# The recurrent branch's Gram products and inverse kept as 64x64 diagonal blocks instead of 128x128 squares

## The chip, the cores and the metric

One Trainium2 chip, one core. The metric is the device time of one execution in microseconds (us), taken as the median of a few runs. TensorE has two clock levels here, 2.4 and 1.2 GHz; a profile gives the granted clock of a stretch as a share of 2.4 GHz.

## The reference

Two different blocks of two layers each, on 256 tokens of width 1024, in float32. The change touches only one branch of the second block's mixer, the recurrent one (`_rwkv7_branch`): eight heads of width 64, each with a 64x64 state that is decayed and updated at every token.

```
def _rwkv7_scan(r, decay, k, v, kk, a):
    def step(state, inp):
        r_t, w_t, k_t, v_t, kk_t, a_t = inp
        sa = jnp.einsum("bhvk,bhk->bhv", state, -kk_t)
        state = (state * w_t[:, :, None, :]
                 + sa[..., None] * (kk_t * a_t)[:, :, None, :]
                 + v_t[..., None] * k_t[:, :, None, :])
        out = jnp.einsum("bhvk,bhk->bhv", state, r_t)
        return state, out
```

Around it, in each of the two layers: one input projection (1024 columns of input, in part for this branch, in part for two convolution branches and for 3072 gate columns), group norm of the branch's output, the gated sum of three branches, an output projection, layer norm, and a feed-forward part (dense in layer 0, a mixture of 8 experts in layer 1). The first block (attention, gates, feed-forward with a convolution) comes before all this and is not touched.

## The kernel before

Weights are streamed in units of 1 MB by SyncE's queue into a ring of buffers. Each engine runs one list of instructions in order, and the engines meet through semaphores: `T.done(...)`, `A.done(...)`, `V.done(...)`, `G.done(...)` count finished work of TensorE, ScalarE, VectorE and GpSimd, and `wait_ge(*V.of("inv", l, p, lv, g))` waits for a certain count. `Z` is one large SBUF tensor that the branch's tiles (`a_`, `b_`, `k_`, `r_`, `gram`, `inv`, `tri`, `off`, `lev`, `xs`, `us`, `state`) are cut from, so a profile calls all of them `Z`. `banks[0..7]` are the eight PSUM banks, all called `bank`.

The recurrence is computed in chunks of 64 tokens. Two chunks make one block `p` of 128 tokens, and there are two blocks (`p` = 0 and 1) in each of the two layers `l`. One block goes through three stages on TensorE (function `rwkv`):

1. **The Gram products** (L841 to L844 and L847). For each head `h` (0 to 7), keys and queries of the 128 tokens are multiplied with each other: four products of 128x128 (contraction over the head's 64 rows) into one bank of 512 columns, and a fifth, L847, which is the transposed one that the inverse starts from. Heads 0, 2, 4, 6 lie in rows 0 to 63 of their tiles and heads 1, 3, 5, 7 in rows 64 to 127. Two banks take turns, so head `h` waits until VectorE has evacuated head `h - 2` (L1931, 512 columns, times a mask that zeroes everything outside the two 64x64 diagonal blocks). L1940 evacuates the fifth product of four heads at a time.
2. **The inverse** of a unit triangular matrix by doubling, in five levels `lv`, for two groups `g` of four heads. GpSimd first prepares it: three operations for each group (L2257, L2259, L2262: 128x512 each) and then `off`, a masked copy of the Gram product for each level (L2268, 128x512). In each level TensorE forms `off.T @ tri` (L862) for both groups; ScalarE copies it out of PSUM into `lev` (L1356, 128x512); TensorE forms `inv.T @ lev` (L870, not in the last level) and `lev.T @ inv` (L873); VectorE adds these to `tri` (L1947) and to `inv` (L1949), 128x512 each. The next level's L862 waits for this.
3. **The chunks**, one after the other (`c` = 0 to 3, two in each block). L893 (with the state) and L895 (with a Gram product) form the right-hand side, ScalarE copies it into `xs`, L901 applies the inverse, VectorE copies that into `us` (L1977), L907 and L908 form the next state, L913 (with the state), L916 and L917 (with Gram products) form the output, which ScalarE copies out (L1374). A chunk's `xs` and `us` are half empty tiles of 128 rows, which is why L1787 clears both at the mixer's start.

TensorE would stand still in much of this, so the projection's remaining units are cut in halves of 16 records (L580, 256 moving columns) and put between: `fill(GRAM_FILL)` (two halves) behind the Gram products, `fill(LEVEL_FILL)` (one half) behind each level, `fill(CHUNK_FILL)` (one half) in each chunk, and fourteen halves before the Gram products. A unit is two halves. ScalarE's list mirrors this: where TensorE's list finishes a unit, ScalarE's waits for it and evacuates it (L1320, 128x512). VectorE's list holds the convolution branch's work between its parts of the levels: `conf_some(3)` puts three taps (six operations, L1862) behind each group's additions in levels 1 to 4 of `p` = 0; in `p` = 1 come the remaining taps, the first block's group norm (L1880 to L1907) and the short convolution.

Around the start of the Gram stage TensorE's list has (L824 forms eight products whose moving side is 2 columns wide):

```
pe.wait_ge(*V.of("bonus", l))
pe.wait_ge(*V.of("rt", l))
pe.wait_ge(*V.of("at", l))
pe.wait_ge(*A.of("tm", l, 5))
for p in range(TB):
    ...
    fill(GRAM_FILL)
    for lv in range(5):
        ...
```

A float32 matmul of the program is two records in the profile (a PE record and a PEld record each time): L862 has 320 records for the 160 matmuls of 2 layers, 2 blocks, 5 levels and 8 heads. A matmul's shape is written as rows*columns of the stationary side, then the moving side.

## Time and profile before

| | us |
|---|---|
| median of 3 runs | 2763.05 (2758.87 to 2769.2) |
| the profiled execution | 2759.35 |
| its span, first to last instruction | 2757.5 |
| TensorE busy | 2632.2 |
| VectorE busy | 1824.5 |
| ScalarE busy | 1260.0 |
| GpSimd busy | 148.8 |

The mean granted clock is 0.981. The three stages of the recurrent branch run from 999.4 to 1179.3 us in layer 0 and from 1572.3 to 1749.4 us in layer 1, so some 360 us of the span.

### The profile page before, as it was taken

The numbers are of one execution on the slowest core, as the hardware profiler recorded it, in microseconds if no ns is written. First come the engines' busy times: TensorE is split into PE (matmuls) and PEld (weight loads), VectorE is DVE, ScalarE is ACT, GpSimd is POOL, SyncE is SP. The second block draws the span as 40 slices with busy tenths as digits, with TensorE's granted clock in tenths as the row PEclk, the third lists the DMA queues.
The fourth block names the chain that finished last, engine by engine and source line by source line (L and its number), as shares of the span: only waits on it lengthen the run. The fifth ranks groups of instructions, "written<-read, shape, count | busy, mean of one in ns | idle before, by whom it ended". The sixth has DMA issues, their size and how long they took to land.

```text
span 2757.5 us, 39119 instructions
## 1 busy us (share of the span) xinstructions
PE 2632.2 (95%) x15410; PEld 2261.3 (82%) x15410; DVE 1824.5 (66%) x2198; ACT 1260.0 (46%) x1443; POOL 148.8 (5%) x125
## 2 busy tenths in 40 slices
PE   7999999999999999999998999889999999999997
PEld 7886998886898888867998888758888888888886
DVE  6654776753777336545545356349889888988988
ACT  4542444451544311113334211127776776777675
POOL 1100000200000021200000023000000000000000
PEclk9999999999999989999998999989999999999999
DMA  6334453333553421135543211249999999999995
GB/s 247 122 138 153 180 189 121 137 139 107 199 183 138 153 77 48 61 122 199 190 169 123 107 62 47 82 188 358 349 356 344 341 358 346 346 359 344 348 357 210
DMA packets 77027, 558.31 MB, mean 202 GB/s; under 512 B 8672, under 2 KB 8800, under 8 KB 9568
## 3 DMA queue, kind: packets, MB, share of 16 engines
q1 hardware_dynamic: 76032, 551.19, 53.6%
q0 software_dynamic: 864, 5.24, 0.5%
q8 instruction: 97, 1.59, 0.2%
q14 instruction: 34, 0.28, 0.0%
HBM read 555.36 MB, written 1.05 MB: 202 GB/s over the span
## 4 chain that ended last, share of the span: by engine, by line
PE 55%; issue 34%; DVE 7%; ACT 2%; POOL 1%; DMA 1%; SPq 0%; POOLq 0%; DVEq 0%; ACTq 0%
PE bank L605 24%; PE bank L628 6%; PE bank L580 6%; PE bank L656 4%; PE bank L590 4%; DVE yT L1862 1%; PE bank L614 1%; PE bank L862 1%; PE bank L873 1%; DMA cst<-in_cst 1%; PE bank L732 1%; PE bank L716 1%; PE bank L715 1%; DVE ring_lo L1584 0%; PE bank L724 0%
## 5 line engine op out<-in xcount | busy, mean ns | idle before, releaser
L2139 DVE TENSOR_TENSOR w_lo<-ring,w_hi 128x2048 fp32r<-128x2048 f32 x216 | 486.3, 2289 | 54.1 <-ACT w_hi L1440 52.9
L1440 ACT ACTIVATE w_hi<-ring 128x2048 fp32r<-128x2048 f32 x216 | 405.1, 1917 | 20.5 <-PE bank L1037 16.7
L1037 PE MATMUL bank<-w_hi,xe_hi 128*128 128x512 f32 x792 | 311.2, 393 | 1.2
L1505 DVE TENSOR_TENSOR w_lo<-ring,w_hi 128x2048 fp32r<-128x2048 f32 x99 | 226.8, 2291 | 127.4 <-ACT w_hi L1136 125.1
L1037 PE MATMUL bank<-w_lo,xe_hi 128*128 128x512 f32 x792 | 308.7, 390 | 0.0
L1037 PE MATMUL bank<-w_hi,xe_lo 128*128 128x512 f32 x792 | 308.3, 389 | 0.0
L605 PE MATMUL bank<-x_hi,w_hi 128*128 128x256 f32 x1056 | 300.4, 284 | 1.5 <-DVE x_lo L1496 1.5
L605 PE MATMUL bank<-x_lo,w_hi 128*128 128x256 f32 x1056 | 300.0, 284 | 0.0
L605 PE MATMUL bank<-x_hi,w_lo 128*128 128x256 f32 x1056 | 299.9, 284 | 0.0
L1136 ACT ACTIVATE w_hi<-ring 128x2048 fp32r<-128x2048 f32 x99 | 189.4, 1913 | 220.4 <-DMA ring<-in_stream 114.8
L580 PE MATMUL bank<-xT,ring 128*128 128x256 f32 x1088 | 251.7, 390 | 1.1 <-ACT Z L1363 1.1
L580 PEld LDWEIGHTS bank<-xT,ring 128*128 128x128 f32 x1088 | 210.5, 196 | 35.0 <-issue 3.4
L605 PE MATMUL bank<-x_hi,ring_lo 128*128 128x256 f32 x832 | 236.9, 285 | 0.0
L605 PEld LDWEIGHTS bank<-x_hi,w_hi 128*128 128x128 f32 x1056 | 203.8, 193 | 3.5 <-DVE x_lo L1496 2.4
L605 PEld LDWEIGHTS bank<-x_lo,w_hi 128*128 128x128 f32 x1056 | 203.9, 193 | 1.1
L605 PEld LDWEIGHTS bank<-x_hi,w_lo 128*128 128x128 f32 x1056 | 203.8, 193 | 0.0
L605 PE MATMUL bank<-x_hi,in_hi 128*128 128x256 f32 x608 | 180.9, 298 | 5.9 <-DVE x_lo L1496 4.5
L1037 PEld LDWEIGHTS bank<-w_hi,xe_hi 128*128 128x128 f32 x792 | 148.6, 188 | 36.5 <-DVE w_lo L2139 6.4
L1037 PEld LDWEIGHTS bank<-w_lo,xe_hi 128*128 128x128 f32 x792 | 148.7, 188 | 31.4
L1037 PEld LDWEIGHTS bank<-w_hi,xe_lo 128*128 128x128 f32 x792 | 148.8, 188 | 30.2
L605 PE MATMUL bank<-x_lo,in_hi 128*128 128x256 f32 x608 | 172.6, 284 | 0.0
L1062 PE MATMUL bank<-w_hi,hT_hi 128*128 128x512 f32 x396 | 163.4, 413 | 0.0
(347 smaller groups left out, 5142.4 us busy)
## 6 DMA issues: line engine op xcount, KB each, us to landing
ring<-in_stream SPq DMA_DIRECT2D x431, 1024.0 KB, 4.9
yT<-in_stream SPq DMA_DIRECT2D x54, 1024.0 KB, 6.2
xT<-in_stream SPq DMA_DIRECT2D x27, 1024.0 KB, 6.6
Z<-in_stream SPq DMA_DIRECT2D x8, 1024.0 KB, 8.7
norm_rows<-in_rows POOLq DMA_DIRECT2D x4, 1024.0 KB, 6.5
cst<-in_cst SPq DMA_DIRECT2D x1, 2145.0 KB, 19.7
par<-in_par SPq DMA_DIRECT2D x1, 1502.0 KB, 15.1
xres<-in_x SPq DMA_DIRECT2D x2, 512.0 KB, 5.9
```

The source lines that it names most:

```text
L580: r = mm(bank[:, c * SEQ:(c + 1) * SEQ], wv[:, k, c * P:(c + 1) * P], xk[:, k, :], start=(k == 0), stop=(k == KT - 1))
L590: r = mm(banks[2 * tb + half], src(c)[:, tb * P:(tb + 1) * P], wv[:, c, half * 512:(half + 1) * 512], start=(first and c == 0), stop=(last ...
L605: r = mm(bank[:, c * SEQ:(c + 1) * SEQ], w[a][:, at], x[b][:, k, :], start=(k == 0 and a == b), stop=(k == KT - 1 and a == 1))
L614: r = mm(bank[:, tb * SEQ:(tb + 1) * SEQ], x[b][:, k, tb * P:(tb + 1) * P], w[a][:, k * 256:(k + 1) * 256], start=(k == 0 and a == b), sto ...
L628: r = mm(banks[2 * tb + half], a[:, j % 2, c, tb * P:(tb + 1) * P], part(b, n)[:, c * D + half * 512:c * D + (half + 1) * 512], start=(j = ...
L656: r = mm(bank[:, half * SEQ:(half + 1) * SEQ], wv[:, k % 2, col:col + P], yk[:, k, :], start=(k == k_at[b]), stop=(k == k_at[b] + splits[b ...
L1037: r = mm(banks[4 + j % 2], a[:, k, :], moe_part(b, i)[:, q * 512:(q + 1) * 512], start=(k == 0 and a is xe_hi and b is w_hi), stop=(k == K ...
L1062: r = mm(banks[half], a[:, j % 2, c * P:(c + 1) * P], moe_part(b, i)[:, c * D + half * 512:c * D + (half + 1) * 512], start=(j == 0 and c ...
L1136: act_(part(w_hi, n), slot(f0 + n), ACT.Copy).then_inc(*A.done("hi", f0 + n))
L1440: act_(moe_part(w_hi, at), moe_slot(at), ACT.Copy).then_inc(*A.done("moe_hi", at))
L1505: v.tensor_tensor(part(w_lo, n), slot(f0 + n), part(w_hi, n).bitcast(F32), ALU.subtract)\
L2139: v.tensor_tensor(moe_part(w_lo, at), moe_slot(at), moe_part(w_hi, at).bitcast(F32), ALU.subtract)\
```

## The change

Outside the two 64x64 diagonal blocks everything that stages 1 and 2 compute is zero. The change keeps a pair of blocks as a tile of 128 rows and 64 columns (rows 0 to 63 the first chunk's block, rows 64 to 127 the second's):

- Stage 1: for each head pair `t`, each of `b_` and `k_`, each chunk `c` and each parity `odd`, one matmul with a 64x64 stationary side and 128 moving columns (64 of `r_`, 64 of `a_`), written to quadrant (rows by parity, output partitions by chunk). Eight heads fill four banks, two heads in each, so VectorE evacuates four times 128x512 (not eight). The transposed products are 16 matmuls of 64*64 with 64 moving columns; they come last and reuse banks 0 and 1, behind a wait for VectorE's first two evacuations; their two evacuations are 128x256.
- Before stage 1 of `p` = 1 TensorE waits for the state of chunk 1 and for ScalarE's copy together; it waited for the state only at the second head.
- Stage 2: `tri`, `inv` and `lev` are 64 columns wide for each head, `off` stays 128 wide and 128x512 for each group. A 128x128 block-diagonal form of `inv` and of `lev` is needed as the stationary side of the other two products, so there are new tiles `inv_wide` and `lev_wide`. Their blocks are copied one at a time (64 rows, 4x64 columns): `inv_wide` at the start by ScalarE (two copies for each group, behind its `fill(GRAM_FILL)`), then by VectorE in levels 0 to 3 (two more additions for each group); `lev_wide` by ScalarE in each level (two copies for each group, next to the one into `lev`). TensorE's first level waits for ScalarE's copies too. `inv` alternates between two buffers. GpSimd's three preparing operations are 128x256.
- Stage 3: the Gram and inverse matmuls take the chunk's 64 rows (64*64) instead of 128 rows with zeros (128*64), with the same 64 moving columns. The matmuls with the state keep all 128 rows (128*64) and 128 moving columns, in the same places between them.
- VectorE's two clearing operations of `xs` and `us` (L1787, 128x512 each) at the mixer's start go; two of 128x1024 (`inv_wide`, `lev_wide`) come just before its part of stage 1, behind its copy of `bonus`. The constants' tensor is 192 columns (98 KB) smaller.

The numbers of fill halves and their places are the same.

```
 # TensorE
-                    for h in range(8):
-                        bs, t = slice(64 * (h % 2), 64 * (h % 2) + 64), h // 2
-                        if h >= 2:
-                            pe.wait_ge(*V.of("gram", l, p, h - 2))
-                        elif p:
-                            pe.wait_ge(*A.of("o", l, 1) if h == 0 else V.of("state", l, 1))
-                            pe.wait_ge(*V.of("us", l, 1))
...
+                    if p:
+                        pe.wait_ge(*A.of("o", l, 1))
+                        pe.wait_ge(*V.of("state", l, 1))
+                        pe.wait_ge(*V.of("us", l, 1))
+                    def quarters():
+                        for c in range(2):
+                            for odd in range(2):
+                                yield c, odd, slice(64 * c, 64 * c + 64), slice(64 * odd, 64 * odd + 64)
+                    for t in range(4):
+                        for wi, w in enumerate((b_, k_)):
+                            for c, odd, ch, bs in quarters():
+                                at = p * P + 64 * c
+                                r = mm(banks[2 * (t // 2) + odd][ch, (t % 2) * SEQ + wi * P:(t % 2) * SEQ + (wi + 1) * P],
+                                       w[bs, t, at:at + 64], r_and_a[bs, :, t * SEQ + at:t * SEQ + at + 64], start=True, stop=True)
+                                if t % 2 and wi and c:
+                                    r.then_inc(*T.done("gram", l, p, t // 2, odd))
+                    for odd in range(2):
+                        pe.wait_ge(*V.of("gram", l, p, 0, odd))
+                    for t in range(4):
+                        for c, odd, ch, bs in quarters():
+                            at = p * P + 64 * c
+                            r = mm(banks[odd][ch, t * 64:t * 64 + 64], a_[bs, t, at:at + 64], b_[bs, t, at:at + 64],
+                                   start=True, stop=True)
...
                     fill(GRAM_FILL)
...
+                                pe.wait_ge(*A.of("inv_wide", l, p, g))
...
-                                r = mm(banks[2 * g][:, (h % 4) * P:(h % 4 + 1) * P], off[:, h, :], tri[:, h, :],
+                                r = mm(banks[2 * g][:, (h % 4) * 64:(h % 4 + 1) * 64], off[:, h, :], tri[:, h, :],
...
-                                    mm(banks[2 * g + 1][:, (h % 4) * P:(h % 4 + 1) * P], inv[:, h, :], lev[:, h, :],
+                                    mm(banks[2 * g + 1][:, (h % 4) * 64:(h % 4 + 1) * 64], inv_wide[:, h, :], lev[:, h, :],
...
+                            pe.wait_ge(*A.of("lev_wide", l, p, lv, g))
...
-                                r = mm(banks[2 * g][:, (h % 4) * P:(h % 4 + 1) * P], lev[:, h, :], inv[:, h, :],
+                                r = mm(banks[2 * g][:, (h % 4) * 64:(h % 4 + 1) * 64], lev_wide[:, h, :], invs[lv % 2][:, h, :],
...
-                                r = mm(dst[:, x * HD:(x + 1) * HD], gram[:, 4 * x + t, 256 + 64 * cc:320 + 64 * cc],
-                                       tm[:, 2, p, t * P + x * HD:t * P + (x + 1) * HD], start=(c == 0), stop=(c == 0 or x == 1))
+                                r = mm(dst[:, x * HD:(x + 1) * HD], gram[ch, 4 * x + t, KA],
+                                       tm[ch, 2, p, t * P + x * HD:t * P + (x + 1) * HD], start=(c == 0), stop=(c == 0 or x == 1))
...
 # ScalarE
                     fill(GRAM_FILL)
+                    for g in range(2):
+                        sc.wait_ge(*G.of("first", l, p, g))
+                        for block, rows in blocks(inv_wide, slice(4 * g, 4 * g + 4)):
+                            act_(block, invs[0][rows, 4 * g:4 * g + 4, :], ACT.Copy).then_inc(*A.done("inv_wide", l, p, g))
...
+                            if lv < 4:
+                                act_(lev[:, hs, :], got, ACT.Copy).then_inc(*A.done("lev", l, p, lv, g))
+                            for block, rows in blocks(lev_wide, hs):
+                                act_(block, got[rows], ACT.Copy).then_inc(*A.done("lev_wide", l, p, lv, g))
...
 # VectorE
-                for buf in (xs, us):
-                    v.memset(buf, 0.0).then_inc(*V.done("zeroed"))
...
+                for wide in (inv_wide, lev_wide):
+                    v.memset(flat(wide), 0.0).then_inc(*V.done("zeroed", l))
...
+                                more = banks[2 * g][:, 0:256].rearrange("p (h n) -> p h n", h=4)
+                                for block, rows in blocks(inv_wide, hs):
+                                    v.tensor_tensor(block, invs[lv % 2][rows, hs, :], more[rows], ALU.add)\
+                                        .then_inc(*V.done("inv_wide", l, p, lv, g))
```

## Rows read from the trace of the kernel before

**Rows 1.** Page, part 1: busy us (share of the span) and instructions
```profile
PE 2632.2 (95%) x15410; PEld 2261.3 (82%) x15410; DVE 1824.5 (66%) x2198; ACT 1260.0 (46%) x1443; POOL 148.8 (5%) x125
```

**Rows 2.** Windows, layer 0: length, busy us (instructions) of each engine, PEclk, DMA
```profile
1000.00:1005.00 5.00, 5.00 (x43) 5.00 (x42) 2.48 (x4) 0.00 (x0) 0.00 (x0) 0.67 0.34 139
...
1040.00:1060.00 20.00, 19.00 (x138) 17.80 (x137) 19.55 (x36) 3.17 (x6) 3.95 (x4) 1.00 0.20 71
...
1107.00:1109.00 2.00, 1.69 (x9) 1.73 (x10) 0.00 (x0) 0.00 (x0) 1.39 (x2) 0.63 0.00 0
```

**Rows 3.** Timeline of TensorE, layer 1, block 0: start, us, instruction, idle
```profile
1572.26 0.49 PE L841 MATMUL bank<-Z 64*128 64x128 f32 x2 [0.27 <-DVE small L1842]
...
1579.85 0.38 PE L847 MATMUL bank<-Z 64*128 64x128 f32 x2
...
1580.16 7.17 PE L580 MATMUL bank<-xT,ring 128*128 128x256 f32 x32
...
1589.64 2.36 PE L862 MATMUL bank<-Z 128*128 128x128 f32 x16 [2.31 <-POOL Z L2268]
```

**Rows 4.** Timeline of TensorE, layer 0, block 1
```profile
1089.88 0.48 PE L841 MATMUL bank<-Z 64*128 64x128 f32 x2 [0.68 <-ACT Z L1374]
...
1090.65 0.27 PE L844 MATMUL bank<-Z 64*128 64x128 f32 x1
...
1091.20 0.38 PE L843 MATMUL bank<-Z 64*128 64x128 f32 x2
...
1097.84 7.17 PE L580 MATMUL bank<-xT,ring 128*128 128x256 f32 x32
...
1107.31 3.56 PE L862 MATMUL bank<-Z 128*128 128x128 f32 x16 [2.29 <-POOL Z L2268]
```

**Rows 5.** Timeline of TensorE, layer 0, block 0
```profile
999.41 0.48 PE L841 MATMUL bank<-Z 64*128 64x128 f32 x2 [0.27 <-DVE small L1842]
...
1010.70 9.46 PE L580 MATMUL bank<-xT,ring 128*128 128x256 f32 x32
```

**Rows 6.** Timelines of GpSimd and ScalarE around stage 1
```profile
1098.31 1.27 POOL L2257 TENSOR_TENSOR Z<-Z,cst 128x512 f32<-128x512 f32 x1 [46.98 <-DVE Z L1940]
...
1587.37 0.60 ACT L1320 ACTIVATE gates<-bank 128x512 f32<-128x512 f32 x1 [16.42 <-PE bank L580]
```

**Rows 7.** Groups of instructions by shape: 256 columns on GpSimd, ScalarE and VectorE
```profile
L2219 POOL TENSOR_TENSOR Z<-Z 128x256 f32<-128x256 f32 x2 | 1.5, 739 | 0.2
...
L1183 ACT ACTIVATE Z<-bank 128x256 f32<-128x256 f32 x2 | 0.7, 364 | 0.0
...
L2148 DVE TENSOR_TENSOR gates<-gates,bank 128x256 f32<-128x256 f32 x99 | 41.1, 415 | 0.0
```

**Rows 8.** Timeline of TensorE: 128-column stationary sides, 2 and 128 moving
```profile
997.30 1.84 PE L824 MATMUL bank<-cst,Z 128*128 128x2 f32 x16
...
1020.00 1.95 PE L862 MATMUL bank<-Z 128*128 128x128 f32 x16
```

**Rows 9.** Timelines of VectorE and TensorE, layer 0, block 0, level 3
```profile
1047.48 0.69 DVE L1947 TENSOR_TENSOR Z<-Z,bank 128x512 f32<-128x512 f32 x1
...
1048.09 0.68 DVE L1949 TENSOR_TENSOR Z<-Z,bank 128x512 f32<-128x512 f32 x1
...
1058.62 1.16 PE L862 MATMUL bank<-Z 128*128 128x128 f32 x8 [0.72 <-DVE Z L1949]
```

**Rows 10.** Timeline of TensorE, layer 0, chunk 2: a tiling change between stages
```profile
1162.27 0.38 PE L908 MATMUL bank<-Z 64*128 64x128 f32 x2
...
1162.59 0.43 PE L913 MATMUL bank<-Z 128*64 128x128 f32 x2
...
1162.86 0.28 PE L916 MATMUL bank<-Z 128*64 128x64 f32 x2
...
1162.97 0.28 PE L917 MATMUL bank<-Z 128*64 128x64 f32 x2
```

**Rows 11.** Chain that ended last, layer 0's mixer start: start, us, what
```profile
884.37 0.48 DVE Z L1787
```

More of the change, by code:

```diff
@@ L148, in const_names @@
                     ("causal", 384), ("window", 384), ("cos64", 256), ("sin64", 256), ("cos32", 256), ("sin32", 256),
-                    ("chunk2", 256), ("earlier", 128), ("slots", 128), ("ones", 128), ("first", 128), ("levels", 6 * 128), ("heads2", 2), ("reset", 256), ("tie", 64)):
+                    ("chunk", 128), ("earlier", 128), ("slots", 128), ("ones", 128), ("first", 64), ("near", 64), ("levels", 5 * 128), ("unit", 64), ("heads2", 2), ("reset", 256), ("tie", 64)):
         n.add(name, w)
@@ L454, in emit, with blocks @@
         rwo = Z[:, 11264:12288].rearrange("p (b n) -> p b n", b=TB)
-        gram = Z[:, 12288:16384].rearrange("p (h n) -> p h n", h=8)
-        inv = Z[:, 16384:17408].rearrange("p (h n) -> p h n", h=8)
-        tri = v_.rearrange("p t n -> p (t n)").rearrange("p (h n) -> p h n", h=8)
+        gram = Z[:, 12288:14336].rearrange("p (h n) -> p h n", h=8)
+        inv_wide = Z[:, 14336:15360].rearrange("p (h n) -> p h n", h=8)
+        lev_wide = Z[:, 15360:16384].rearrange("p (h n) -> p h n", h=8)
+        invs = [x.rearrange("p (h n) -> p h n", h=8) for x in (Z[:, 16384:16896], v_.rearrange("p t n -> p (t n)")[:, 512:1024])]
+        lev = Z[:, 16896:17408].rearrange("p (h n) -> p h n", h=8)
+        tri = v_.rearrange("p t n -> p (t n)")[:, 0:512].rearrange("p (h n) -> p h n", h=8)
         off = Z[:, 17408:18432].rearrange("p (h n) -> p h n", h=8)
-        lev = Z[:, 18432:19456].rearrange("p (h n) -> p h n", h=8)
+        r_and_a = Z[:, 0:12288].rearrange("p (x n) -> p x n", x=2)
+        BR, BA, KR, KA = (slice(64 * i, 64 * i + 64) for i in range(4))
+        def blocks(wide, hs):
+            return [(wide[64 * c:64 * c + 64, hs, 64 * c:64 * c + 64], slice(64 * c, 64 * c + 64)) for c in range(2)]
         xs = Z[:, 19456:19968]
@@ new lines, in rwkv @@
+                    for odd in range(2):
[5 more added lines that the diff above has]
+                                   start=True, stop=True)
+                            if t == 3 and c:
+                                r.then_inc(*T.done("m", l, p, odd))
@@ new lines, in mixer @@
+                    for pair in range(2):
+                        for odd in range(2):
+                            ve.wait_ge(*T.of("gram", l, p, pair, odd))
+                            if p:
+                                ve.wait_ge(*T.of("o", l, 1))
+                            at = 4 * odd + 2 * pair
+                            v.tensor_tensor(gram[:, at:at + 2, :].rearrange("p h (w n) -> p (h w) n", w=2),
+                                            banks[2 * pair + odd].rearrange("p (q n) -> p q n", q=4),
+                                            grow(ct("chunk"), [P, 4, P], 1), ALU.mult).then_inc(*V.done("gram", l, p, pair, odd))
@@ L1942, in mixer @@
+                    for g in range(2):
+                        ve.wait_ge(*T.of("m", l, p, g))
+                        if p == 0 and g == 0:
+                            ve.wait_ge(*A.of("tm", l, 1))
+                        v.tensor_tensor(tri[:, 4 * g:4 * g + 4, :], banks[g][:, 0:256].rearrange("p (h n) -> p h n", h=4),
+                                        grow(ct("first"), [P, 4, 64], 1), ALU.mult).then_inc(*V.done("first", l, p, g))
                     for lv in range(5):
@@ L2255, in mixer @@
                             po.wait_ge(*V.of("ends", l))
-                        ident4 = grow(ct("ident"), [P, 4, P], 1)
+                        ident4 = grow(ct("unit"), [P, 4, 64], 1)
                         g.tensor_tensor(tri[:, hs, :], tri[:, hs, :], ident4, ALU.add).then_inc(*G.done("tri1", l, p, gg))
-                        g.tensor_tensor(inv[:, hs, :], gram[:, hs, 0:P], grow(ct("levels", 0, P), [P, 4, P], 1), ALU.mult)\
+                        inv = invs[0]
+                        g.tensor_tensor(inv[:, hs, :], gram[:, hs, BA], grow(ct("near"), [P, 4, 64], 1), ALU.mult)\
                             .then_inc(*G.done("inv1", l, p, gg))
@@ L2330, in level @@
         return ((lo // (2 * n) == hi // (2 * n)) & (lo % (2 * n) < n) & (hi % (2 * n) >= n)).astype(f)
-    c["first"] = level(1, j, i)
-    c["levels"] = np.concatenate([level(n, i, j) for n in (1, 2, 4, 8, 16, 32)], 1)
+    narrow = lambda m: m[:, 0:64] + m[:, 64:128]
+    c["first"] = narrow(level(1, j, i))
+    c["near"] = narrow(level(1, i, j))
+    c["levels"] = np.concatenate([level(n, i, j) for n in (2, 4, 8, 16, 32)], 1)
+    c["unit"] = narrow((i == j).astype(f))
     c["heads2"] = (i[:, 0:2] // 64 == j[:, 0:2]).astype(f)
```

57 lines of the change are left out of this document (16 added, 41 removed).

## The prediction

> **What bounds the kernel now.** I read the page first: TensorE is busy for 2632 of 2757.5 us [rows 1]. So where its list runs without a gap, only less work on TensorE shortens the time, and elsewhere only the wait that ends last. Then I read the recurrent branch in windows, in time order on each engine, and along the chain that ended last. The reader should see three regimes. Around stage 1 the gap in front of level 0 is ended by GpSimd: 2.31 and 2.29 us [rows 3, 4]. (In layer 0's block 0 the clock hides it, below.) In levels 1 to 4 of block 0 VectorE is busy for 19.55 of 20 us and TensorE waits for it, 0.72 us in front of the last level's second group [rows 2, 9]; so it is in levels 0 to 2 of block 1 by the same timeline. The chunks are one chain with TensorE in nearly all of it. The fill halves are work that has to be done somewhere, so I move them and never save them.
>
> I use five paces, all in records (two for a float32 matmul). A pair of records with a 64*128 stationary side and 128 moving columns takes 0.22 us, 0.111 each. Sixteen records of 128*128 with 128 moving take 1.95 us, the last one's 0.28 included: again 0.111 [rows 8]. Sixteen of 128*128 with only 2 moving columns take 1.84 us, so 0.106 each [rows 8]: with next to nothing to stream, a 128-column stationary side still costs 0.106. With 64-column stationary sides and 64 moving it is 0.056 (L916 to L917, two records in 0.11 us) [rows 10]. And where two heads in different row halves stand next to each other, eight records pass between 1090.65 and 1091.20, 0.069 each against 0.111 [rows 4]: the halves do overlap.
>
> **Stage 1, pace.** Before: 80 records for a block. After: 64 with 128 moving columns and 32 with 64. Every next matmul is in the other row half, so I take a perfect overlap of two: 64 x 0.0555 = 3.55 us and 32 x 0.029 = 0.93 us, 4.5 in all. Bounds: 1.8 + 0.5 us if all four quadrants overlap; 7.1 + 1.8 = 8.9 us if nothing does. The trace has two partners at once and never four, so I take two. VectorE keeps up: its evacuations of 512 follow one another in 0.60 us [rows 9]; pair 0 at 1.9 to 3.2, pair 1 at 3.75 to 5.0, the first 256-wide one done at 5.4. Its two new 128x1024 clearings fall into the 1.9 us before the first evacuation and into idle time before it.
>
> The Trainium skill, page "TensorEngine Tiling (Array Packing)", section Key Properties, says that different tiles load and multiply in parallel, and lists four tiles for 64x64. By that rule stage 1 would take 2.3 us in place of 4.5; no row here shows more than two.
>
> **Stage 1 to level 0.** GpSimd: from its start at 1098.31 to TensorE's at 1107.31 seven operations of 512 take 9.0 us [rows 4, 6]. A 256-wide one took 0.739 us [rows 7], pitch 0.70, so six of them with two own waits take 4.3, and `off` 1.25: 5.45 + 4.3 + 1.25 + 0.15 = 11.15 us after stage 1 began. TensorE has 4.5 + 0.1 (tiling change, below) + 7.17 of fill [rows 3] = 11.8 us. GpSimd is no longer last; its gap goes.
>
> In block 0 something takes its place. ScalarE's list has its own `fill(GRAM_FILL)` ahead of the new `inv_wide` copies. Fourteen halves went before, so these two complete a unit with their last record: its evacuation starts at 1587.37, right at the fill's end [rows 6]. Level 0 then waits 0.6 us for it and for two copies of 64x256 (0.364 each) [rows 7]: 1.4 us with the hand-overs. In block 1 seven more halves lie between, the unit ends in the middle of the fill, and the copies are long done.
>
> - Layer 1, block 0: 17.4 us from 1572.26 to 1589.64 [rows 3]; after, 11.8 + 1.4 = 13.2. L862's sixteen records took 2.36 there against 1.95 [rows 3, 8]. Gain 4.2 + 0.4 = 4.6.
> - Layer 0, block 0: the clock fell in it (mean 0.67 from 1000 to 1005 us) [rows 2]; before, TensorE had done the products of two columns. I assume the same fall, 1.9 us in. 34 records by then, 30 x 0.111 + 32 x 0.058 = 5.2 after, the fill begins at 1006.5 and takes the same 9.4 us [rows 5]: 1015.9 + 1.4 = 1017.3 against 1020.00 [rows 8]. Gain 2.7. With full clock it would be 6 more.
> - Block 1, both layers: 17.4 us [rows 4]; after, 11.8 plus 0.55, since the first product now waits for the last of four state operations. Gain 5.1. Behind the 2.29 us gap the clock was down (0.63 in 1107 to 1109) [rows 2], and L862 took 3.56 against 1.95 [rows 4, 8]; without the gap I give back 1.6. Together 6.7, twice: 13.4.
>
> Sum of this part: -20.7 us.
>
> **Levels.** The moving side is halved, but `off`, `inv_wide` and `lev_wide` are stationary sides of 128 columns. Bounds: 0.056 and 0.111 a record. The nearest row is that of 2 moving columns, 0.106, so I take 0.106: 48 records save 0.24 us in a level, and in eight of the twenty levels TensorE sets the pace: -1.9. VectorE: additions of 512 have a pitch of 0.60 against a duration of 0.69 [rows 9]; a 256-wide one lasts 0.415 [rows 7], so pitch 0.33. Four of these (1.32) replace two of 512 (1.20): +0.12 for each group, and in twelve groups of each layer VectorE sets the pace: +2.9. ScalarE's three copies (1.1 us) instead of one (0.6) are hidden: `lev` is sooner ready, and L870's eight records (0.85) cover the wide copies; in the last level it has 0.85 us for two copies of 0.73. If that cover went, each level would cost up to 0.5 more. GpSimd's `off` is unchanged and still overlaps VectorE's taps.
>
> **Chunks.** Numbers of records and columns stay, so contraction over 64 rows saves nothing. But the tiling does not stay: in chunks 1 to 3 the state products are 128*64 and the Gram products between them become 64*64. L908 (64*128) starts at 1162.27 and lasts a pair's 0.22; L913 (128*64) starts at 1162.59, 0.10 late, and its own pair takes 0.27 instead of 0.22 [rows 10]. A change of rows alone, L847 to L580, costs 0.09 (1579.85 + 0.22 against 1580.16) [rows 3]. Four alternations in each of two stages are 14 new changes for a chunk, 84 in six chunks. Bounds: 0 (if this one pair of tilings mixed freely, which no row excludes) and 0.15. I take 0.15, since every change seen costs: +12.6. All of it lies on the chain, as nothing else waits there but TensorE's own order.
>
> The Trainium skill, same page and section, says that a change of tiling mode, though not one of tile, drains TensorE. By that rule, the rows above agree, with 0.10 us a time.
>
> **Mixer start.** The two clearings of `xs` and `us` (0.48 each, 0.51 with the gap) stand on the chain in front of the first split [rows 11]. ScalarE's high part is ready at about the same time as they start, so I give back 0.95 in each layer: -1.9. The smaller constants I count at nothing.
>
> **Sum.** -20.7 - 1.9 + 2.9 + 12.6 - 1.9 = -9.0 us against the profiled execution's 2759.35. That execution is 3.7 us under the median of the three runs, 2763.05; against the median I forecast 2754.
>
> **Rivals.**
> 1. Four quadrants overlap. Level 0 then starts 10.3 us after stage 1 began instead of 11.8 (VectorE and GpSimd follow close behind): 1.5 us four times and 1 more in the slow stretch, 2747. For it: the quadrants share no row-and-column pair. Against it: only pairs seen. The Trainium skill's rule on tiles, named above, is this case.
> 2. 128*64 and 64*64 mix without a cost: 12.6 less, 2741. For it: both have 64 columns. Against: the change of rows alone cost 0.09.
> 3. The levels run at the moving side's pace: 48 x 0.05 - 0.24 = 2.2 us in eight levels, 2737. Against it: the 0.106 row.
> 4. Slower: the clock. In the levels the array would stream for about half of each record's 0.106 us; if the granted clock falls to 1.2 GHz there as it did at 1001 and 1107 us [rows 2], a level costs 5.1 us more. From five levels on the kernel is slower; in the eight that TensorE paces it would be +41, 2795. Against it: fill stands behind nearly every level, and the chunks' 64-column products, with as few columns in flight, kept the full clock by the same timelines.
> 5. The quadrants give nothing, one after another: +4.4 us four times and some 2 more in the slow stretch, 2774. Against it: [rows 4].
> 6. The change does not shorten GpSimd's preparation (256-wide operations as long as 512-wide): level 0 starts at 14.5 us, +2.7 twice and +1.3 twice, 2762.
>
> **Chances and range.** My forecast 0.48, rivals in order 0.18, 0.08, 0.05, 0.06, 0.10, 0.05. What a measurement here can tell is 0.5%, 13.8 us: under 2749.2 is faster, over 2776.9 slower. Faster: 0.15 of the forecast, two thirds of rival 1, all of rivals 2 and 3: 0.32. Slower: rival 4 mostly and a quarter of rival 5: 0.07. Same: 0.61. Leaving out rivals 3 and 4 and the far edge of rival 5, the range is 2740 to 2771.
>
> **What would show it.** Right: no idle time ended by GpSimd before level 0; in block 0 an idle of about 1.4 us ended by ScalarE; from stage 1's start to level 0 some 12 to 13 us; L862, L870 and L873 of 128*128 with 64 moving at 0.106 a record; steps of 0.15 us wherever 128*64 meets 64*64. Wrong: level records at 0.056, a stage 1 under 3 us, chunks as long as before, or a granted clock near 0.5 in the levels.

## The result, and the profile after

The changed kernel takes 2800.3 us (median of four runs, 2793.27 to 2802.6); before took 2764.8 beside it (2758.87 to 2769.2). The ratio is 1.0126, with a 95% interval of 1.0098 to 1.0153: slower by some 35 us, where the prediction had 9 us less and put the end of its range at 2771. The profiled execution of after is 2793.27 us with a span of 2791.5, 34.0 more than the span of before, and its mean granted clock is 0.965 against 0.981. It is the fastest of the four (the other three have 0.960 or 0.961), so the stretches below show rather too little of the loss than too much.

The page of after, part 1 and the clock row of part 2, answers to [rows 1]; the last line is the clock row of before:

```profile
PE 2661.6 (95%) x15474; PEld 2270.1 (81%) x15474; DVE 1818.6 (65%) x2246; ACT 1282.2 (46%) x1531; POOL 135.3 (5%) x125
...
PEclk9999999999999998899999988889999999999999
...
PEclk9999999999999989999998999989999999999999
```

TensorE does the same fill and fewer columns, and is busy for 29 us more. The clock row says where to look: it has six 8s where before has three, and the new ones stand in the two places where the recurrent branch runs (a digit is some 70 us). So I cut the branch of each layer into three kinds of stretch: from stage 1's first record to level 0's, the five levels, and the two chunks of a block. Each is the difference of two start times, of both layers and both blocks together. (In block 1 the stretch of chunks is taken from its first Gram record. The state product ahead of it, 0.3 us in before and 0.4 in after, stands with the levels.)

| stretch | before | after | change | predicted for it |
|---|---|---|---|---|
| stage 1 to level 0 | 72.8 | 47.9 | -24.9 | -17.1 |
| levels | 182.8 | 198.0 | +15.2 | -2.6 |
| chunks | 101.3 | 138.9 | +37.6 | +12.6 |
| all else | | | +6 | -1.9 |

(Of the prediction's -20.7 for stage 1, 3.6 were for records of the first level, so they stand in the second row here.) "All else" is 3.0 us ahead of layer 0, -1.4 between the two layers and 4.4 behind the second. Layer 0's stage 1 starts anywhere from 999.2 to 1008.1 us in the traces of this study, whatever was changed in them, so the first figure says nothing about this change. Some 2 of the last 4.4 are the clock again, which stays down behind the last chunk: the four records that follow it (L941) take 3.78 us, in before (L922) 1.98. The other 2 are not explained.

The stretches of layer 0 in the windows of after; then narrower ones, around the places where the clock falls (length, busy us and instructions of TensorE, its weight loads, VectorE, ScalarE and GpSimd, granted clock, DMA share and GB/s). They answer to [rows 2]; the last line is the stretch of block 0's chunks in before:

```profile
1002.45:1015.26 12.81, 9.78 (x129) 8.35 (x129) 4.82 (x8) 1.54 (x4) 6.69 (x8) 1.00 0.22 79
1015.26:1064.55 49.29, 47.88 (x304) 44.99 (x304) 34.13 (x81) 11.50 (x32) 10.02 (x8) 0.90 0.17 63
1064.55:1097.63 33.08, 29.26 (x209) 23.70 (x209) 6.11 (x16) 2.97 (x5) 0.00 (x0) 0.79 0.09 33
...
1108.79:1159.98 51.19, 46.97 (x300) 43.57 (x298) 37.05 (x68) 14.58 (x34) 13.52 (x10) 0.90 0.13 49
1159.98:1195.17 35.19, 32.26 (x224) 24.96 (x223) 3.90 (x8) 2.37 (x4) 0.00 (x0) 0.82 0.08 30
...
1071.00:1073.00 2.00, 1.74 (x15) 1.74 (x16) 0.21 (x1) 0.00 (x0) 0.00 (x0) 1.00 0.95 389
1073.00:1075.00 2.00, 2.00 (x20) 1.88 (x20) 1.13 (x4) 0.00 (x0) 0.00 (x0) 0.58 0.25 102
1033.00:1036.00 3.00, 1.59 (x14) 1.45 (x12) 2.90 (x8) 1.62 (x4) 1.27 (x1) 0.96 0.58 177
1036.00:1044.00 8.00, 8.00 (x38) 8.00 (x38) 6.29 (x14) 1.03 (x3) 1.27 (x1) 0.50 0.16 68
...
1065.18:1089.88 24.70, 21.55 (x208) 19.26 (x209) 6.04 (x16) 2.96 (x5) 0.00 (x0) 1.00 0.12 44
```

Block 0's chunks take 33.08 us at a mean of 0.79. In before the same stretch takes 24.7 us at 1.00; by the same windows, before's clock is 1.00 in every stretch of chunks of both layers. That is the finding of this study, and everything below asks what pulls the clock down.

The timeline of TensorE, after, layer 0: stage 1 of block 0 up to level 0 (it answers to [rows 3, 5]), level 2's second group, chunk 0, and the x stage of chunk 2; the last two lines are the x stage of chunk 2 in before (start, us, instruction, idle time before it and what ended that):

```profile
1002.45 1.98 PE L855 MATMUL bank<-Z 64*64 64x128 f32 x64 [0.27 <-DVE small L1866]
1005.83 0.69 PE L864 MATMUL bank<-Z 64*64 64x64 f32 x32 [1.40 <-DVE Z L1959]
1006.46 7.17 PE L589 MATMUL bank<-xT,ring 128*128 128x256 f32 x32
1015.26 1.97 PE L880 MATMUL bank<-Z 128*128 128x64 f32 x16 [1.62 <-ACT Z L1375]
...
1035.37 1.62 PE L880 MATMUL bank<-Z 128*128 128x64 f32 x8 [1.41 <-DVE Z L1979]
1036.78 1.91 PE L888 MATMUL bank<-Z 128*128 128x64 f32 x8
...
1069.28 1.14 PE L920 MATMUL bank<-Z 64*64 64x64 f32 x16
1071.26 0.48 PE L926 MATMUL bank<-Z 64*128 64x128 f32 x2 [0.84 <-DVE Z L2007]
...
1073.24 0.43 PE L935 MATMUL bank<-Z 64*64 64x64 f32 x2
1073.46 0.42 PE L936 MATMUL bank<-Z 64*64 64x64 f32 x2
...
1159.62 0.43 PE L912 MATMUL bank<-Z 128*64 128x128 f32 x2
1159.98 0.44 PE L914 MATMUL bank<-Z 64*64 64x64 f32 x4
1160.35 0.43 PE L912 MATMUL bank<-Z 128*64 128x128 f32 x2
...
1153.59 0.39 PE L893 MATMUL bank<-Z 128*64 128x128 f32 x2
...
1154.04 0.39 PE L893 MATMUL bank<-Z 128*64 128x128 f32 x2
```

Four things to read. First, stage 1's 64 records pass in 1.98 us, a pitch of (1.98 - 0.27) / 63 = 0.027 us: four quadrants at once. Level 0 begins 12.81 us after stage 1, behind an idle time ended by ScalarE's copies. Second, a chunk's stages: the pair L935, L936 has a pitch of 0.21 us, 0.107 a record, where [rows 10] had two records of the same number of columns in 0.11. That is not a change of tiling, since chunk 0 has none between these two: it is the clock, at 0.58 in that window. Third, a change of tiling has its own price: a step from one L912 to the next, four records of L914 and two changes between them, is 0.73 us where before has 0.45 from one L893 to the next for as many records, 0.14 for each change. Fourth, eight records of L888 take 1.91 us in the window at 0.50 and 1.06 at full clock.

VectorE of after just ahead of level 2's second group (level 1's additions for it), the timeline (it answers to [rows 9]):

```profile
1033.66 0.42 DVE L1973 TENSOR_TENSOR Z<-Z,bank 128x256 f32<-128x256 f32 x1
1034.00 0.86 DVE L1977 TENSOR_TENSOR Z<-Z,bank 64x256 f32<-64x256 f32 x2
1034.89 0.42 DVE L1979 TENSOR_TENSOR Z<-Z,bank 128x256 f32<-128x256 f32 x1
1035.23 3.77 DVE L1886 SCALAR_TENSOR_TENSOR yT<-Z,par,yT 128x252 f32<-128x252 f32 x6
```

The group now occupies VectorE from 1033.66 to 1035.23, 1.57 us, where two additions of 512 took 1.21 [rows 9] (from 1047.48 to its next start at 1048.69). The two additions of 64 partitions take 0.43 each, as long as one of 128 partitions: half the partitions save nothing.

ScalarE and GpSimd of after around level 0 of block 0, the timeline:

```profile
1007.29 0.73 POOL L2287 TENSOR_TENSOR Z<-Z,cst 128x256 f32<-128x256 f32 x1 [62.99 <-DVE Z L1966]
...
1013.67 0.60 ACT L1339 ACTIVATE gates<-bank 128x512 f32<-128x512 f32 x1 [12.53 <-PE bank L589]
1014.16 1.72 ACT L1375 ACTIVATE Z<-Z 64x256 f32<-64x256 f32 x4
```

GpSimd's 256-wide operation is 0.73 us and no gap ends with it any more. ScalarE evacuates the fill's unit at the fill's very end, and only then makes the four copies on which level 0 waits.

### The profile page after: what moved, and what is told of

It reads as the page before. It is cut to its first block and busy times, and to the rows that moved or that the text cites. A ratio compares the mean times of both kernels' runs of the same rounds, so it can differ in the third digit from the quotient of the medians.

```text
span 2791.5 us, 39399 instructions
## 1 busy us (share of the span) xinstructions
PE 2661.6 (95%) x15474; PEld 2270.1 (81%) x15474; DVE 1818.6 (65%) x2246; ACT 1282.2 (46%) x1531; POOL 135.3 (5%) x125
```

## Experiments

Two theories stood at first. **The array theory:** TensorE's clock falls where its records use a small part of the array, here the chunks' 64*64 products (A in the expectations); with 128 rows in each product the chunks would go back to full clock. **The other theory (B):** the chunks cost only their changes of tiling, some 12.6 us, and the rest of the loss comes out of the levels. The first two experiments put that part of the change into before, and take it out of after.

**Chunk products on 64 rows, in the kernel before.**

```
-  r = mm(dst[...], gram[:, 4 * x + t, 256 + 64 * cc:320 + 64 * cc], tm[:, 2, p, ...])
+  r = mm(dst[...], gram[ch, 4 * x + t, 256 + 64 * cc:320 + 64 * cc], tm[ch, 2, p, ...])
...
-  r = mm(banks[1][ch, ...], inv[:, 4 * (h % 2) + h // 2, ch], xs[:, ...])
+  r = mm(banks[1][ch, ...], inv[ch, 4 * (h % 2) + h // 2, ch], xs[ch, ...])
...
-  mm(d, gram[:, ..., 128 + 64 * cc:192 + 64 * cc], us[:, hv]); mm(d, gram[:, ...], tm[:, 2, p, hv])
+  mm(d, gram[ch, ..., 128 + 64 * cc:192 + 64 * cc], us[ch, hv]); mm(d, gram[ch, ...], tm[ch, 2, p, hv])
```

> The kernel before with stage 3 alone changed: the Gram and inverse matmuls of the chunks take the chunk's 64 rows (64*64) in place of 128 (128*64). Theory A (small tiles): a chunk of 64*64 matmuls makes the granted clock fall by itself, as it fell in chunk 0 of the changed kernel, where nothing changes its tiling; then this kernel shows the clock near 0.5 from the first chunk on, and is slower than before by about 38 us (12.6 for 84 tiling changes, some 25 for the clock): 2803. Theory B (the clock falls because the shorter stage 1 and the levels' waits leave gaps, and stage 3 costs only its tiling changes): the clock stays at 1.0 in the chunks and the kernel is slower by about 13 us: 2778.

2812.49 us against 2765.35, ratio 1.0166 (1.0145 to 1.0187): 47 us slower from a change of row slices alone, 9 more than the array theory's figure, and slower than the whole change. The levels stay as they were (45.2 and 46.2 us in layer 0, at 1.00 and 0.96). The windows of its chunks of block 0, and the timeline of TensorE in chunk 0:

```profile
1069.35:1103.79 34.44, 31.28 (x209) 25.13 (x209) 6.04 (x16) 2.96 (x5) 0.00 (x0) 0.72 0.08 31
```

```profile
1074.05 1.14 PE L901 MATMUL bank<-Z 64*64 64x64 f32 x16
1076.03 0.48 PE L907 MATMUL bank<-Z 64*128 64x128 f32 x2 [0.84 <-DVE Z L1977]
...
1077.03 0.38 PE L907 MATMUL bank<-Z 64*128 64x128 f32 x2
...
1077.49 0.64 PE L907 MATMUL bank<-Z 64*128 64x128 f32 x2
```

The fall can be watched here: the same form of instruction takes 0.38 us, and half a microsecond later 0.64. Ahead of it stand sixteen 64*64 records, a wait of 0.84 and some 64*128 records. The following stretch pays too: stage 1 of block 1 takes 21.2 us at a clock of 0.74, where before has 17.4 at 1.00.

**After with the chunk products on 128 rows.** The reverse of the diff above, on the changed kernel's tiles; the kernel leaves out keeping the two chunks' products apart.

> The changed kernel with the chunks' Gram and inverse matmuls back on 128 rows (128*64), and the clearing of xs and us back. The compact tiles hold both chunks' blocks, so these products mix the two chunks: the output is not the reference's, the work on every engine has the shape of a correct kernel. Theory A: the chunks keep the full clock and take 24.7 and 26.2 us in layer 0 as before instead of 33.1 and 35.6, and the kernel is about 38 us faster than the changed one: 2762, level with before. Theory B: only the tiling changes go, the clock still falls in the chunks: 2787.

2768.05 us against 2765.35, ratio 1.0011 (1.0000 to 1.0022). That is 32 us less than after: the array theory, by 6 us off its figure. The windows are worth more than the sum: the chunks are at 25.4 and 25.9 us and 1.00 in layer 0, but now the levels of block 1 take 56.9 and 58.2 us at 0.79 and 0.77. So there is a second fall, in the levels, and it moves about: the levels of block 0 are at 1.00 in layer 0 (46.3 us) and at 0.90 in layer 1 (49.3 us) of this one execution. Nor do 128 rows rule the fall out. The chunks of block 0 in layer 1:

```profile
1635.07:1663.45 28.38, 24.56 (x209) 22.25 (x209) 6.10 (x16) 2.96 (x5) 0.00 (x0) 0.88 0.11 38
```

The clock is at 1.00 up to 1641 us there and falls behind the wait of 0.84 and the state products, where the chunks of after lose it too.

**State products first, so that fewer tilings alternate.** The stages x and o issue their four 128*64 products ahead of all Gram products: one change in a stage and not seven. A third theory (C) was at stake, that the alternation brings the clock down.

```
+  if c:
+      for t in range(4):
+          mm(banks[0][ch, t * P:(t + 1) * P], a_[:, t, tc_], state[:, t, :], start=(t == 0), stop=False)
   for t in range(4):
       dst = banks[0][ch, t * P:(t + 1) * P]
-      if c:
-          mm(dst, a_[:, t, tc_], state[:, t, :], start=True, stop=False)
```

> The changed kernel with the four state products of a stage put ahead of its Gram products instead of between them: 12 of the 14 new tiling changes of a chunk go, 72 in all; the same matmuls. Each change is worth 0.15 us, so -10.8 us: 2789, with the clock falling in the chunks as before (theory A, the size of the tiles). If instead it is the tiling changes with their drains that bring the clock down (theory C), the clock stays up in chunks 1 to 3 as well and the kernel comes to about 2770.

2786.5 us against 2765.35, ratio 1.0082 (1.0065 to 1.0099). 14 us less than after, where 72 changes at 0.14 are 10. The third theory falls: with hardly a change left, block 0's chunks still stand at 32.1 us and 0.75.

**Stage 1 with the row halves apart.** All products of one row half first, then the other: no two neighbours in different row halves.

```
-  for t in range(4):
-      for wi, w in enumerate((b_, k_)):
+  for want in range(2):
+      for t, (wi, w) in [(t, q) for t in range(4) for q in enumerate((b_, k_))]:
           for c, odd, ch, bs in quarters():
+              if odd != want:
+                  continue
```

> The changed kernel with stage 1's 64 records of one block in another order: all of rows 0 to 63 first, then all of rows 64 to 127, so neighbours differ only in the output partitions. If four quadrants work independently and only neighbours overlap, the pitch is 0.056 us a record (3.6 us in all, instead of 0.027 and 1.7). If column halves do not overlap by themselves and the four-way pace came from a deep queue, it is 0.111 (7.1 us).

One execution, 2817.87 us. TensorE's timeline, block 0:

```profile
1003.30 3.34 PE L857 MATMUL bank<-Z 64*64 64x128 f32 x64 [0.27 <-DVE small L1868]
```

(3.34 - 0.27) / 63 = 0.049 us a record, against 0.027 with four quadrants and 0.111 for a 64*128 stationary side [rows 4]. Two column halves overlap without the row halves, which the expectation had a little slower. Level 0 of block 0 still starts at 12.8 us, since ScalarE's copies come last; but the clock is down in block 1's stage 1 (15.5 us at 0.68, after has 11.2 at 0.87) and in its levels (58.4 us at 0.77). Less of the array in use at a time, and again the clock; but this is one execution, and the levels' 64 moving columns lose the clock without this edit too.

**Levels with 128 moving columns.** If a half-streamed 128-column stationary side is what brings the clock down in the levels, then streaming the 64 columns twice must mend it, although it is twice the columns. The second copy goes to bank columns that nothing reads.

```
-  r = mm(banks[2 * g][:, (h % 4) * 64:(h % 4 + 1) * 64], off[:, h, :], tri[:, h, :], ...)
+  r = mm(banks[2 * g][:, (h % 4) * P:(h % 4 + 1) * P], off[:, h, :], grow(tri[:, h, :], [P, 2, 64], 1), ...)
```

and likewise for `inv_wide` by `lev` and `lev_wide` by the inverse, the readers taking every other 64 columns.

> The changed kernel with each of the levels' three products streaming its 64 moving columns twice (128 moving columns, the second copy's result unused; the readers take the first). The pitch of a record should stay 0.111 us, as the stationary side sets it. If the clock falls in the levels because the array streams only about half of each record's time, the four level stretches (49.3, 51.2, 46.3, 51.2 us) come to about 46 each with the clock at 1.0: 2785 to 2790. If it falls because of the waits for VectorE there, or carries over from the chunks, nothing changes: 2800.

2779.18 us against 2764.7, ratio 1.0058 (1.0040 to 1.0077): 21 us less than after for twice the moving columns in the levels. Its timeline at the place where after's clock fell at 1035 us:

```profile
1032.12 1.16 PE L880 MATMUL bank<-Z 128*128 128x128 f32 x8 [1.40 <-DVE Z L1979]
1033.12 1.06 PE L888 MATMUL bank<-Z 128*128 128x128 f32 x8
```

The wait ahead is the same (1.40 against 1.41, for the same addition), the records are the same in number and stationary side, and L888's eight take 1.06 us here and 1.91 in after. One such pair would prove little, for after's own layer 1 has the same records behind the same wait and keeps the clock:

```profile
1619.70 1.10 PE L880 MATMUL bank<-Z 128*128 128x64 f32 x8 [1.41 <-DVE Z L1979]
1620.64 1.06 PE L888 MATMUL bank<-Z 128*128 128x64 f32 x8
```

It is the count over all traces that decides. With 64 moving columns the levels of block 0 have a mean clock of 0.90 in eight of ten stretches (after, no_s3, grouped, rows_apart, act_first) and 1.00 in two; with 128 moving columns (this kernel and the five below that keep the edit) they have 1.00 in all twelve. In block 1 it is 0.76 to 0.90 against 0.93 to 1.00. So 64 moving columns make the fall likely behind these waits, not certain. Nor are 128 proof against it: in block 1 of this kernel, behind a wait of 3.58 us, the clock is 0.71 from 1124 to 1126 us. And at full clock the 64 moving columns have given nothing: L888's eight take 1.06 in either kernel.

**The same, with the chunk products on 128 rows too.**

> The same on the kernel with the chunks back on 128 rows (output not the reference's: the two chunks' products are mixed). Its level stretches were 46.3, 56.9, 49.3 and 58.2 us against 46 each before. If the moving columns are what holds the clock, they come to 46 each and the whole gain of stage 1 shows: 2765 - 25 = 2740. If the waits are the cause: 2768.

2744.5 us against 2764.7, ratio 0.9923 (0.9905 to 0.9940). With both edits undone, stage 1's gain is left: 20 us. The predicted gain of stage 1 was real. Seven of its eight stretches of levels and chunks in question are at 0.96 or above; the chunks of block 1 in layer 1 are at 0.94, with a fall behind the state products again.

**Idle twins.** The change keeps the diagonal blocks alone, so the chunks' products stay at 64 rows and the array must be filled in another way. Each Gram product of x and o gets a neighbour in the opposite quadrant (the other rows, the other columns), whose output nobody reads, on top of the two edits above (128 moving in the levels, state products first). No run has those two alone, so what the twins add to the whole kernel is an estimate: 2779.2 less grouped's 13.8 would be 2765.

```
   for x in range(2):
+      ot = slice(64 - 64 * cc, 128 - 64 * cc)
+      mm(banks[1][ot, ...], gram[ot, 4 * x + t, KA], tm[ot, 2, p, ...], start=True, stop=True)
       r = mm(dst[...], gram[ch, 4 * x + t, KA], tm[ch, 2, p, ...], ...)
```

> lev128, the state products grouped ahead, and beside each 64*64 Gram product of the chunks' x and output stages an idle twin of the same size in the opposite quadrant (other row half, other output partitions, a free bank; its result is unused). If the quadrants overlap as in stage 1, the twins cost little (0 to 2 us in a chunk); if the clock falls in the chunks because only a quarter of the array works, it falls less or not at all: 2760 to 2770. If the clock does not depend on that share, it stays down and the kernel is at 2775 or above.

2754.76 us against 2764.7, ratio 0.9963 (0.9949 to 0.9977). Block 1's chunks are at 25.8 us and 1.00. Block 0's are not (30.3 at 0.83), and the windows say why:

```profile
1066.00:1068.00 2.00, 1.16 (x13) 1.02 (x12) 0.68 (x1) 0.00 (x0) 0.00 (x0) 1.00 0.71 238
1068.00:1070.00 2.00, 2.00 (x22) 1.78 (x21) 0.38 (x2) 0.00 (x0) 0.00 (x0) 0.71 0.68 287
1070.00:1072.00 2.00, 2.00 (x42) 2.00 (x42) 0.74 (x3) 0.00 (x0) 0.00 (x0) 0.50 0.03 8
```

The clock falls behind the inverse's records and the state products, which have no twins yet.

**A fill half in place of twins.** On the same two edits, half a unit of fill between the state update and o, one in each chunk; they are taken from the fourteen halves ahead of the Gram products (thirteen now) and from behind the last chunk.

```
   r.then_inc(*T.done("s", l, c))
+  fill(1)
```

> lev128, the state products grouped ahead, and one more fill half in each chunk, between the state's and the output's products, taken from the halves that ran before stage 1 and behind the last chunk. The work is the same. If a stretch of small tiles without full-array work in it makes the clock fall, a fill half in its middle keeps it up: 2755 to 2765. If the small tiles bring it down whatever stands between: about 2775.

2760.65 us against 2764.7, ratio 0.9985 (0.9975 to 0.9995). Block 0's chunks are at 1.00 (33.0 us, with two more fill halves of 3.6 us in them), block 1's at 0.86 (37.9 us). Fill that would have to be done anyway can hold the clock too, though here only in one block of two. That small tiles bring the clock down whatever stands between them is ruled out by block 0.

**Twins for the inverse and the state products too.**

```
   for h in range(8):
+      mm(banks[3][ot, h * 64:h * 64 + 64], invs[1][ot, h, :], tm[ot, 2, p, h * 64:h * 64 + 64], ...)
       r = mm(banks[1][ch, h * 64:h * 64 + 64], invs[1][ch, 4 * (h % 2) + h // 2, :], xs[ch, ...], ...)
...
+  for x in range(2):
+      mm(banks[1][:, two], tm[ot, x, p, two], tm[ot, 2, p, two], start=True, stop=True)
   mm(dst, tm[ch, 0, p, two], us[ch, two], start=True, stop=False)
```

> The kernel twins, with idle twins in the opposite row half also beside the inverse products (64*64) and the state products (64*128) of each chunk. In twins the clock still fell in chunks 0 and 1, behind these two stages (30.3 us instead of 25.4 at full clock). If it is the array's idle part that brings the clock down, it stays up now: 26 us in chunks 0 and 1, a microsecond less in the levels of block 1, 2745 in all. If it is the waits between the stages (0.84 us before the state products), the chunks stay at 30 us: 2755.

2746.86 us against 2763.25, ratio 0.9939 (0.9924 to 0.9954). The windows of its chunks, block 0 and block 1 of layer 0, and the timeline of the inverse's records:

```profile
1059.77:1085.73 25.96, 22.09 (x369) 19.49 (x369) 6.03 (x16) 2.97 (x5) 0.00 (x0) 1.00 0.11 42
1145.24:1171.27 26.03, 23.06 (x377) 20.31 (x376) 3.89 (x8) 2.38 (x4) 0.00 (x0) 1.00 0.11 42
```

```profile
1064.60 0.22 PE L925 MATMUL bank<-Z 64*64 64x64 f32 x1
1064.61 0.22 PE L927 MATMUL bank<-Z 64*64 64x64 f32 x1
1064.66 0.22 PE L925 MATMUL bank<-Z 64*64 64x64 f32 x1
1064.67 0.22 PE L927 MATMUL bank<-Z 64*64 64x64 f32 x1
...
1066.50 0.37 PE L934 MATMUL bank<-Z 64*128 64x128 f32 x1 [0.85 <-DVE Z L2020]
```

Twin and product start 0.01 us apart, at a pitch of 0.06 for the two: the twins take no time. With 369 instructions in place of 209 the stretch takes 25.96 us in place of 33.08, and the wait of 0.85 in front of the state products is there as before. All four stretches of chunks are at 1.00. This version beats both kernels, before by 0.6%.

**ScalarE's copies ahead of its fill list**, on the kernel above and on after itself:

```
   for p in range(TB):
-      fill(GRAM_FILL)
       for g in range(2):
...
+      fill(GRAM_FILL)
       for lv in range(5):
```

> twins_all with ScalarE's copies into inv_wide moved ahead of its fill(GRAM_FILL): level 0 of block 0 no longer waits behind the evacuation of the unit that ends there. Stage 1 of block 0 comes down from 12.8 to 11.2 us in both layers (3.2 us in all), and nothing else moves: 2742. If GpSimd is right behind, it stays at 12.5 or above.

2747.3 us against 2763.25, ratio 0.9941 (0.9926 to 0.9957).

> The changed kernel with only that move of ScalarE's copies. Stage 1 of block 0 in 11.2 instead of 12.8 us twice: 2797. By the clock's chances in the chunks the total may differ by some microseconds either way.

2793.8 us against 2763.25, ratio 1.0103 (1.0082 to 1.0124). In both, level 0 of block 0 starts at 11.0 us and not 12.8, so the wait for ScalarE is named rightly and gone. The total does not show it. On twins_all it is 4.2 us less in the branch by the profiled executions, while the medians differ by 0.4 the other way. In those two executions layer 0's stage 1 starts 3.3 us later and the way between the layers is 2.2 us longer, two places that differ from trace to trace anyway; more is not known of the 4.2 us. In after (the intervals of 1.0103 and 1.0126 overlap) the clock falls elsewhere instead: block 0's chunks go from 33.1 to 30.6 us at 0.89, and block 1's from 35.2 to 38.9 at 0.71.

**All traces together.** The mean clock of a stretch of chunks (two layers, two blocks, in each kernel):

| Gram and inverse products of the chunks | stretches | at 1.00 | the others |
|---|---|---|---|
| 128 rows (before, no_s3, lev128_no_s3) | 12 | 10 | 0.88, 0.94 |
| 64 rows (after, s3_only, grouped, rows_apart, lev128, act_first) | 24 | 0 | 0.70 to 0.89 |
| 64 rows, twins beside Gram, inverse and state products (twins_all, twins_all_act) | 8 | 8 | |
| 64 rows, twins beside the Gram products alone (twins) | 4 | 2 | 0.83 |
| 64 rows, one more fill half in each chunk (spread) | 4 | 2 | 0.86 |

## Why the prediction was wrong, by its own steps

**The step that failed** is the chunks' cost, +12.6 us where the runs have +37.6, with its sentence in rival 4: that the chunks' 64-column products, with as few columns in flight, kept the full clock. They did, in before, with 128 rows (1.00 in all four stretches). The change makes the same products 64*64, a quarter of the array in place of half, and the prediction's sum treated that edit as one that saves nothing and costs only changes of tiling. The runs showed a fall to 1.2 GHz there: 47 us from this edit alone in the kernel before, 32 us back when it alone is undone in after. The rival was named, at 6 in 100, but placed in the levels; most of it was in the chunks.

- **Changes of tiling:** right in size. 0.14 us each against 0.15 taken; 84 make 11.8 of the chunks' 37.6 us. The other 26 are in the main the clock, which twins without any useful work bring back (with the alternation gone too, the chunks from their very first record are 106.0 us against 139.6 in after).
- **Stage 1, pace:** rival 1 was right on the mechanism: 0.027 us a record against 0.0555 taken, a quarter of the 0.111 of one record after the other. The Trainium skill, page "TensorEngine Tiling (Array Packing)", section Key Properties, says that different tiles can load and multiply in parallel; the trace agrees with 0.027. But stage 1 then waits 1.40 us for VectorE's first evacuations, so only a part arrives: 12.8 and 11.2 us to level 0 against 13.2 and 12.35. (Block 1's 11.2 are at a clock of 0.87; at 1.00 it takes 10.3 in no_s3, rival 1's figure.)
- **Stage 1, layer 0, block 0:** mis-sized by 5.1 us. I assumed before's fall of the clock in it; it did not come (1.00 in all of it), and 20.6 us became 12.8. The sum has a slip here: its own terms give 4.7 us more at full clock (1017.3 against 999.4 + 13.2), not 6.
- **ScalarE takes the place of GpSimd in block 0:** right, 1.62 us against 1.4, and gone when its list is reordered.
- **Levels, TensorE:** 0.111 us a record whatever the moving side, against 0.106 taken; the saving of 1.9 is nothing.
- **Levels, VectorE:** mis-sized. +0.36 us for a group and not +0.12: 64-partition additions take 0.43 us, and the next one waits. 24 groups make 8.6 us at the most; with the clock mended (lev128), the levels are 190.1 us, 7.2 over before, where the prediction had 2.6 under. One place has most of that: in front of level 2's second group in block 1 TensorE waits 3.58 us where before has 0.92, since VectorE's four taps ahead of that group's additions start 1.0 us later and take 4.77 us instead of 3.64.
- **Levels, clock:** 198.0 against those 190.1, so 7.9 us of after's loss (and 21.8 where the chunks alone are on 128 rows: 210.7 us of levels against 188.9 with 128 moving columns as well). Rival 4's place and mechanism, in fewer levels than it took.
- **Block 1's 1.6 us back behind the gap:** right at its place. In level 0 of block 1 the first product's records take 1.90 us until the next product starts (1108.79 to 1110.69) where before has 3.34 (1107.31 to 1110.65), and the clock there is 1.00. It is lost again in level 2, where after falls to 0.56 (1131.1 to 1133.1) behind the wait of 3.58 us. The levels of block 1 have a mean of 0.96 in before and in lev128 alike, but from different falls: behind GpSimd's gap in the one, behind that wait in the other.
- **Mixer start:** 392.96 us between the layers in before, 391.61 in after: 1.35 less against 0.95, with other kernels of this study from 391.6 to 394.8 (spread, whose fill is placed otherwise, aside). Not told apart.

What is shown and what is argued: shown is that the row cut in the chunks and the halved moving columns in the levels each cost what the runs say (32 and 21 us when undone one at a time, 56 together), and that they do it through the clock (the table, and the count under lev128). The waits are the same with and without the fall (1.40 us with 128 or 64 moving columns; 0.85 with or without twins), so the waits alone are not the cause; but each of the falls shown here starts within some microseconds behind a wait, so no trace shown here has a fall without one. A fall in one stretch can last into the next, as in stage 1 of block 1 of s3_only; why the same row cut costs 47 us in before and 32 in after stays open, as does why no_s3's levels in block 1 are 6 us slower than after's. What in the records the clock follows is not settled: rows, columns and moving columns each changed it, and no run separates them. Nor is it the same every time: like stretches of one execution differ (46.3 us at 1.00 and 49.3 at 0.90). Splitting the state products into 64*64 halves was not tried.

## What to carry to other kernels

A smaller tile is not a cheaper one: before a contraction is cut to the rows that are not zero, ask what else works in the array at that moment, since TensorE at 100% busy can run at half its clock. If nothing does, keep the zeros, or put a matmul in the free quadrant; neither cost time here. And price a split by the partitions and columns that an operation is charged for: half the partitions on VectorE, or half the moving columns under a 128-column float32 stationary side, save nothing here. Last, one pair of rows from two traces is no proof of what the clock does: count the stretches of all of them.

## What was not expected of the hardware

- The granted clock falls while TensorE is busy without a gap: 2.00 of 2.00 us busy at 0.58 (after, 1073 to 1075), behind 64*64 and 64*128 records; a wait of 0.84 us stands 2 us ahead.
- A second matmul in the opposite quadrant is free (0.06 us for a pair of records, as for one), and with it the clock held at 1.00 in eight stretches of chunks out of eight.
- Column halves overlap as row halves do: 0.049 us a record with the row halves apart, 0.027 with all four quadrants.
- VectorE's taps take far longer while GpSimd's `off` operations run beside them: four of 227 columns 4.77 us at 1124.66 of after (3.64 in before), four of 229 columns 1.68 us at 1117.54, with GpSimd idle. TensorE waits 3.58 us for what is behind them.
